# A decoder step with a paged cache: four keys of a page in each of 32 partitions, in place of one key in each of 128

## What is computed

```python
k_all = concatenate([pool_k[page_table].reshape(b, past, h, e), k_new], axis=1)      # pages of 128 keys
v_all = concatenate([pool_v[page_table].reshape(b, past, h, e), v_new], axis=1)
lf_all = concatenate([pool_logf[page_table].reshape(b, past, h), logf_new], axis=1)
c = cumsum(lf_all, axis=1)
sc = einsum('bthe,bshe->bhts', q, k_all) * scale + cq - ck                            # cq, ck: c at the query, at the key
p = softmax(sc); out = einsum('bhts,bshe->bthe', p, v_all)
```

## Time and profile before

| | us |
|---|---|
| median of three timed runs | 1434.57 |
| lowest and highest of them | 1431.95 and 1443.98 |
| the profiled execution's own time | 1441.41 |
| its span, first to last instruction | 1439.8 |

### The profile page before, as it was taken

How to read it: one execution, slowest core, us unless ns; L and a number is a source line. 1 busy time by engine, 2 the same in 40 slices (tenths; PEclk the granted TensorE clock), 3 DMA queues, 4 the chain that set the end, 5 groups by cost and what they waited for, 6 DMA issues and landing times.

```text
span 1439.8 us, 25872 instructions
## 1 busy us (share of the span) xinstructions
PE 1371.4 (95%) x9293; PEld 1237.6 (86%) x9293; DVE 964.1 (67%) x1386; ACT 553.1 (38%) x908; POOL 253.9 (18%) x304
## 2 busy tenths in 40 slices
PE   6999999977898999989999999999999999999999
PEld 4778887856676766689989999999999999999999
DVE  6758889976775566665887888788878887311111
ACT  6423121164444455554355444443444355201010
POOL 5540025332221134110011101110111000000000
PEclk9899999988886589999999999999999999999999
DMA  8248765677885677433222221222122257232222
GB/s 281 61 138 262 226 192 170 197 220 219 255 237 157 212 217 218 126 114 118 74 82 81 89 82 59 81 89 81 59 82 89 89 178 267 77 105 74 83 72 70
DMA packets 192314, 200.99 MB, mean 140 GB/s; under 512 B 24661, under 2 KB 167406, under 8 KB 191778
## 3 DMA queue, kind: packets, MB, share of 16 engines
q1 hardware_dynamic: 165596, 153.75, 34.5%
q0 software_dynamic: 9776, 29.96, 6.8%
q10 hardware_dynamic: 16814, 15.62, 3.5%
HBM read 169.47 MB, written 29.82 MB: 138 GB/s over the span
## 4 chain that ended last, share of the span: by engine, by line
PE 70%; DVE 12%; issue 6%; DMA 5%; POOL 3%; ACT 1%; SPq 1%; ACTq 1%; POOLq 0%; DVEq 0%
PE ps L1288 8%; PE ps L1289 8%; PE ps L1290 8%; PE ps L1349 5%; PE ps L1350 5%; PE ps L1351 5%; PE ps L1127 4%; PE ps L1027 2%; PE ps L1152 2%; PE ps L1028 2%; PE ps L1029 2%; PE ps L1109 2%; PE ps L1094 2%; PE ps L1131 1%; DMA upr<-in_w_upL 1%
## 5 line engine op out<-in xcount | busy, mean ns | idle before, releaser
L1288 PE MATMUL ps<-hhi,uph 128*128 128x258 f32 x704 | 200.8, 285 | 4.0 <-issue 1.4
L1289 PE MATMUL ps<-hlo,uph 128*128 128x258 f32 x704 | 199.6, 284 | 0.0
L1290 PE MATMUL ps<-hhi,upl 128*128 128x258 f32 x704 | 199.3, 283 | 0.0
L1027 PE MATMUL ps<-whi,hhi 128*128 128x512 f32 (+1 forms) x376 | 145.1, 386 | 12.7 <-DVE wlo L1865 8.3
L2581 DVE TENSOR_TENSOR dnl<-dnr,dnh 128x896 fp32r<-128x896 f32 (+2 forms) x24 | 27.3, 1136 | 172.3 <-ACT dnh L1778 172.3
L1029 PE MATMUL ps<-whi,hlo 128*128 128x512 f32 (+1 forms) x376 | 142.5, 379 | 0.0
L1028 PE MATMUL ps<-wlo,hhi 128*128 128x512 f32 (+1 forms) x376 | 142.3, 379 | 0.0
L1288 PEld LDWEIGHTS ps<-hhi,uph 128*128 128x128 f32 x704 | 133.8, 190 | 5.5 <-DVE ug L2539 1.7
L1289 PEld LDWEIGHTS ps<-hlo,uph 128*128 128x128 f32 x704 | 134.1, 191 | 0.0
L1290 PEld LDWEIGHTS ps<-hhi,upl 128*128 128x128 f32 x704 | 133.8, 190 | 0.0
L2759 POOL TENSOR_TENSOR upr<-upr 128x512 f32<-128x512 f32 x22 | 29.6, 1345 | 450.0 <-DMA upr<-in_w_upL 373.5
(11 more groups left out here) (335 smaller groups left out, 3657.9 us busy)
## 6 DMA issues: line engine op xcount, KB each, us to landing
upr<-in_w_upL SPq DMA_DIRECT2D x88, 256.0 KB, 3.4
ring<-in_cache_a_k SPq DMA_DIRECT2D x168, 128.0 KB, 2.7
vring<-in_cache_a_v POOLq DMA_DIRECT2D x128, 128.0 KB, 3.3
vring<-in_cache_a_v SPq DMA_DIRECT2D x104, 128.0 KB, 3.0
scr_act<-va SPq DMA_DIRECT2D x22, 516.0 KB, 2.6
ring<-in_cache_a_k ACTq DMA_DIRECT2D x88, 128.0 KB, 2.8
wst<-in_w_in SPq DMA_DIRECT2D x32, 256.0 KB, 3.9
fr<-scr_act SPq DMA_DIRECT2D x14, 516.0 KB, 5.5
```

Of the source, the lines that this page charges most:

```text
L1027: pe.matmul(out, lh, whi[:, sl, 0:w], start=(kc == 0), stop=False)
L1288: pe.matmul(out, hi_, r_hi[:, cs], start=(first and i == 0), stop=False, skip_group_check=not first)
L1289: pe.matmul(out, hi_, r_lo[:, cs], start=False, stop=False, skip_group_check=not first)
L1290: m = pe.matmul(out, lo_, r_hi[:, cs], start=False, stop=(i == 3), skip_group_check=not first)
```

## The change

`load_pages` writes page j of a granule to the 32 partitions j, j + 4, j + 8 and so on. Each takes four keys in a row, 4 KB, so partition 4p + j holds keys 4p to 4p + 3 of page j. This holds for key and value pages on all three queues. A granule still fills 128 partitions x 4 KB. The order of the keys in `sA` changes with it, so the bias has to lie in the same order: ACT now copies it into a new tile `bias_k` (in the place of a scratch tile that is free by then), and sixteen DMAs from SBUF to SBUF, issued by SP at unit (2, 3), take 32 partitions x 1 KB each from `bias_k` to `biasA`. Their arrival is counted on `const_ld`, on which `forget_bias` now waits too. The bias add reads `biasA` in an order permuted within the partition.

```diff
--- before.py
+++ after.py
@@ -201,7 +201,8 @@
         sqt0 = at("sqt0", [P, 516], f32, u10_0 + 4096)[0]
         lfp = at("lfp", [P, 2, PSZ * NH], f32, sq_end)[0]
         bias0 = o
-        biasA, o = at("biasA", [P, 8, PAGES, NH], f32, o)
+        biasA, o = at("biasA", [P, 4, 8 * PAGES // 4, NH], f32, o)
+        bias_k = at("bias_k", [P, 4, 8 * PAGES // 4, NH], f32, pidx_end)[0]
         oS = at("oS", [NSAMP, 4, WG], f32, bias0)[0]
         qb, o = at("qb", [P, 8, WG], f32, o)
         ring, o = at("ring", [P, 4, 4, WG], f32, o)
@@ -391,6 +392,7 @@
                 K_AT[u_].append(n_)
                 n_ += 1
         assert n_ == NKP
+        BIAS_AT = (2, 3)
         K_ASK = {u: [n + 4 for n in K_AT.get(u - 1, ()) if n + 4 < NKP] for u in range(NU)}
         NKA = NSAMP * PAGES // 4
 
@@ -403,7 +405,8 @@
 
             for j in pages:
                 page = sp.value_load(ptab[0:1, bass.ds(seq * PAGES + (group * 4 + j), 1)], min_val=0, max_val=NPOOL - 1)
-                sp.dma_start(dst[:, slot, j, :], pool[bass.ds(page, 1)].rearrange("o p c -> p (o c)"))\
+                sp.dma_start(dst[j:P:4, slot, :, :].rearrange("p r c -> p (r c)"),
+                             pool[bass.ds(page, 1)].rearrange("o (p r) c -> p (o r c)", r=4))\
                     .then_inc(S(f"{sem}{slot}"), 16)
 
 
@@ -627,6 +630,12 @@
                     sp.wait_ge(S("x_sq"), 3 * KC)
                     for s4 in range(4):
                         load_pages(sp, kpool, 0, s4, s4)
+                if k == BIAS_AT:
+                    sp.wait_ge(S("lft_cp"), 4)
+                    for q in range(4):
+                        for r in range(4):
+                            sp.dma_start(biasA[q:P:4, r].rearrange("p g h -> p (g h)"),
+                                         bias_k[r:P:4, q].rearrange("p g h -> p (g h)")).then_inc(S("const_ld"), 16)
                 if k == (2, 2):
                     for s4 in range(4):
                         uses = [m for m in prompt_no if prompt_no[m] % 4 == s4 and m[0] in (0, 5)]
@@ -1433,8 +1442,8 @@
                 for i in range(2):
                     act.wait_ge(S("lft_pe"), 8 + i + 1)
                     for b4 in range(4):
-                        v = ps[:, 4 + i, :].rearrange("p (h b g) -> p b g h", h=NH, b=4)[:, b4]
-                        m = act.activation(biasA[:, 4 * i + b4], v, ACT.Copy)
+                        v = ps[:, 4 + i, :].rearrange("p (h b g q) -> p b q g h", h=NH, b=4, q=4)[:, b4]
+                        m = act.activation(bias_k[:, :, 8 * (4 * i + b4):8 * (4 * i + b4) + 8, :], v, ACT.Copy)
                     m.then_inc(S("lft_cp"), 1)
 
             for u, k in enumerate(units):
@@ -2051,8 +2060,9 @@
             def forget_bias(half):
                 T_.wait("k_used", 32 * (half + 1))
                 T_.wait("lft_cp", 4)
-                v = sA[:, 4 * half:4 * half + 4].rearrange("p b g h -> p (b g h)")
-                link(dve.tensor_tensor(v, v, biasA[:, 4 * half:4 * half + 4].rearrange("p b g h -> p (b g h)"), ALU.add))
+                v = sA[:, 4 * half:4 * half + 4].rearrange("p b (g r) h -> p (b g) r h", r=4)
+                T_.wait("const_ld", 336)
+                link(dve.tensor_tensor(v, v, biasA[:, :, 32 * half:32 * half + 32, :].rearrange("p r g h -> p g r h"), ALU.add))
 
             def early_softmax():
```

## The result

| | before | after |
|---|---|---|
| median, us | 1433.26 (4 runs, 1426.89 to 1443.98) | 1460.24 (4 runs, 1455.04 to 1468.24) |
| ratio, 95% interval | | 1.0182 [1.012, 1.0245] |
| profiled execution, us | 1441.41 (span 1439.8) | 1455.04 (span 1453.4) |

The changed kernel is slower, by 27 us in the medians. Executions of one kernel lie up to 17 us apart here, the longer ones with a lower granted clock, and the profiled one before, 1441.41 us, is among the longer of its kernel while the one after, 1455.04, is the shortest of its four. So the 13.6 us between the two profiles are not the loss; it is read from the medians, and from when a given piece of work is done. The profile does not point at one place at once, so here are its views in the order of the rows before. The first is the granted clock, part 2 of the page, against the earlier trace rows.

What follows compares the result with a forecast made beforehand. PE was taken as the bound, at half speed in group M, late pages costing their wait and then some half-speed us. Terms -0.6 - 1.4 + 2.6 + 0.2 = +0.8 us on 1434.57 gave 1435.4 us, range 1409 to 1443.

Steps and rivals of the forecast that it cites:

- part 1: Page loads with 4 KB rows for 1 KB: -0.6 us at page waits, -1.4 us at the qb load, issue saving nothing.
- C: Projection near 172 us: PE's wait for the bias DMAs is followed by a clock fall, +3.5 us, 1438.9; chance 0.20.
- D: Page transfers: 32 rows run at half the rate, at least 72 us more, about 1511; chance 0.03.
- the 0.2 us that it allowed: Sign of a right forecast: page landings stay within 0.2 us of those before the change.
- The 0.08 us: Page loads: each page lands 0.08 us sooner with 4 KB rows, taken from estimates of 0.06 and 0.10 us.
- the sign of under half on both: Sign of a right forecast: under half as many packets on the queues of SP and ACT.
- A: Attention: pages land much earlier and the clock rises with them, -16 us, 1418.6; chance 0.24.
- E: Page transfers: 4 KB rows are cut into 1 KB packets, so no gain from longer rows, 1437.4; chance 0.05.
- the seven waits: Pieces of the wait chain, 257.97 to 556.32 us, read as ending on page arrivals; 0.08 us saved each, -0.6 us.
- Part 2: Sixteen bias DMAs in the projection hold SP 5.8 us, DVE waits 4.2, PE's spatial mixing 2.6; +2.6 us.
- Part 3: Bias copies on ACT cost 0; DVE's bias add, 0.68 us twice, grows 0.1 us each, +0.2 us in all.
- The clock from 430 to 512: Group M of the attention: TensorE's clock, 0.59 before, was forecast to be low again from 440 to 512 us.

Runs made afterwards that it cites:

- the run of the layout alone: Changed kernel without the sixteen bias DMAs, forget bias left in its old order; 1.0161 of the kernel before, again 1.0151 in another job.
- relieved SP: 24 value-page issues moved from SP to POOL: 0.9895 in the kernel before, 1.0034 in the changed kernel, both relative to the kernel before.
- page numbers first: A group's page numbers read before its issues: 0.9974 in the kernel before; 1.0131 in the changed kernel with its bias DMAs on POOL.
- side by side run: Changed kernel with page j in adjacent partitions 32j to 32j + 31, bias DMAs on SP writing 32 adjacent partitions; 1.0105 of the kernel before.

## Why the prediction was wrong

1435.4 us was forecast, within 1409 to 1443; it became 1460.24.

- **The step that failed:** part 1's "a saving of at most 0.04 us in about 1.1 us per page", of which it says "I count it as nothing". I argued from the number of rows. The step over partitions, which no page DMA of the kernel before has, made the issue 473 ns: no saving but 0.135 us more per page. The runs showed in its place that six waits of about this length, with the pages in their old form, cost as much as the layout (1.0144 and 1.0151 in one job). A form of issue that the trace does not show needed a bound on the side of a loss, and had none.
- **And what it stood on:** I never asked whether SP has time left. From 293 to 430 us SP waited 5.0 of 137 us. In group A before the change it issued 56 key and 37 value pages; 93 issues of 0.135 us are 12.6 us, an estimate, and group A became 10.9 us longer. Ahead of group A the first sixteen pages took 2.25 us longer in a row, and by the run of the layout alone the pages are 6.9 us of the later start (306.2 for 299.3). None of the five rivals had this mechanism; of C and D, which had the sign, one was on the bias DMAs and the other on the transfers.
- **Part 1, the landings:** right for the most part. 2.6 and 3.4 us for 2.7 and 3.3; SP's and ACT's value pages, 0.3 and 0.4 us later, are outside the 0.2 us that it allowed. The 0.08 us that each page was to land sooner show nowhere. ACT's packets fell to 0.36; SP's, which carry other loads too, only to 0.85, against the sign of under half on both. Both falls are what rows of 4 KB in one packet make: 96 packets fewer per page are 10,752 on ACT's queue, as measured, and 26,112 on SP's, where it was 25,344 with the bias DMAs' new rows among them. Rivals A, D and E fall by that. Of the seven waits one was misread: at 516.13 PE itself stood still for 0.57 of the 4.66 us; and D's price adds up to 1509 and not 1511.
- **Part 2:** the mechanism was right link by link, the size was off. Forecast 16 x 0.36 = 5.8 us of SP, 4.2 us for DVE, 2.6 for PE; measured 11.2, 9.88 and 8.74, with a half-speed clock for some 3.5 us behind it, as C had it. The term mis-sized is the 0.36, which is 0.70: I took a dense issue for one that steps over partitions. Alone it is 0.4%, with an interval that reaches down to no loss; beside a relieved SP the part ahead of the attention, of which it is about half, is what remains.
- **Part 3:** the add took 0.682 us for 0.68; my +0.2 was 0.
- **The clock from 430 to 512:** forecast low as before; it was 0.87. (0.87 - 0.59) x 73 us of busy time are 20 us given back in the profiled execution, an estimate, which fits that the key products end 28.8 us later and the last value sums of the cache only 12.8 (583.8 for 571.0). It need not be the change that gave them back: with page numbers first in the kernel before, the attention starts at 299.6 and the key products end at 422.9, both within 1 us of before, and this clock is 0.81. In both the clock falls behind the qb load; before it stood at 0.50 for most of 450 to 512 us, there it was at 1.00 again from 460 to 480. Over the experiments it lay between 0.63 and 0.85, and where one kernel's executions part into shorter and longer, the profiled one with 0.63 or 0.65 is among the longer (1439.41 in 1418.62 to 1442.24; 1462.60 in 1446.20 to 1462.60), as 1441.41 with 0.59 is. What decides it stays open. The forecast took it from that one execution for a property of the kernel.

## What to carry to other kernels

Before costing a DMA edit, look how long its issuing engine waits for anything: a queue engine that hardly waits (here 5.0 of 137 us) is a bound, though no busy share shows it, and then each issue's own time is on the path. Look for bursts too: sixteen pages in a row held up four weight loads in a stretch where SP waited 42 us. A DMA whose SBUF side steps over partitions was dearer to issue on SP and ACT than one over a dense block (473 for 338 or 321 ns); packets per page and bytes say nothing of that. Where SP is the bound, moving issues to an engine with time left was worth more than the change of the transfers' form: 24 of them gave about 1%. And compare a relieved kernel with a relieved one: against the kernel before, the changed one seemed to have lost only 0.3%.

## What was not expected of the hardware

- The issue of a page went from 338 to 473 ns on SP and from 344 to 488 on ACT, for steps of two and four alike (475 and 491 for two), 64 or 32 partitions, and not at all on POOL (546 to 538; 555 for a step of two). On a block of 32 it was 321.
- DMAs that stand directly behind such a page on SP also took longer: the outputs of a unit had 0.43 us, and 0.58 behind a page; loads of the memory keys 434 ns and then 584.
- Sixteen DMAs from SBUF to SBUF with a step on either side took 0.60 us each to issue on SP and 0.70 from one to the next; with the step on one side only (source, side by side run) still 0.59. On POOL 0.54.
- Three, six and twelve fulfilled waits a page cost 0.05, 0.16 to 0.19 and 0.40 us: more than in proportion at first. What sets this stays open.
